# The expert layer of 128 of the 512 tokens by gathered expert rows, the dense expert passes on the other 384

## What is computed

```
q = (xt @ w_query).reshape(T, PEER_HEADS, 2, PEER_HALF)
s = einsum('thpd,pkd->thpk', q, sub_keys)             # scores of 2 x 128 keys
s_top, i_top = lax.top_k(s, K)                        # K = 16
cand = s_top[..., 0, :, None] + s_top[..., 1, None, :]
best, pos = lax.top_k(cand, K)                        # 16 experts of each head
eidx = index of the chosen pair (first key * 128 + second key)
g = softmax(best)
u = expert_u[eidx]                                    # rows, [T, heads, K, 1024]
a = gelu(einsum('thkd,td->thk', u, xb))
w = g * a
out = einsum('thk,thkd->td', w, expert_v[eidx])
```

## Time and profile before

| | us |
|---|---|
| median of three runs | 3341.32 |
| the profiled execution | 3339.1 |
| its span, first to last instruction | 3337.3 |
| stage A, from the trace | about 219 |
| stage W | about 465 |
| stage C | about 131 |
| between the passes | about 11 |
| stage V | about 705 |

### The profile page before, as it was taken

One profiled execution on the slowest core, in us unless ns is written; L12 is line 12 of the kernel. 1 busy time (PEld: TensorE's weight loads), 2 busy tenths in 40 slices (PEclk: granted clock), 3 DMA queues, 4 the chain that ended last, 5 costly groups with the idle time before them and its releaser, 6 DMA issues.

```text
span 3337.3 us, 38272 instructions
## 1 busy us (share of the span) xinstructions
PE 3069.8 (92%) x13740; PEld 2417.3 (72%) x13740; DVE 2045.0 (61%) x3267; ACT 1018.7 (31%) x1298; POOL 20.1 (1%) x19
## 2 busy tenths in 40 slices
PE   3966889999999999989999999769999998899997
PEld 2653458888888888878888888548887783478885
DVE  5456748975666663244444444487777647468886
ACT  3211434333333333232222222222222326322222
POOL 0001000000000000000000000000000000100000
...
GB/s 193 82 110 145 29 52 64 133 145 141 169 176 189 180 184 176 176 189 183 195 184 192 201 183 188 94 26 94 94 94 89 88 89 1 32 70 95 99 96 51
DMA packets 130786, 414.75 MB, mean 124 GB/s; under 512 B 7696, under 2 KB 73616, under 8 KB 98448
## 3 DMA queue, kind: packets, MB, share of 16 engines
...
## 4 chain that ended last, share of the span: by engine, by line
PE 87%; DVE 8%; ACT 2%; DMA 1%; issue 1%; POOL 0%; SPq 0%; ACTq 0%; DVEq 0%
PE ps L332 26%; PE ps L336 25%; PE ps L335 25%; PE ps L1793 3%; PE ps L1552 2%; PE ps L1970 1%; DVE sb_stats L1484 1%; DMA sb_stage<-w_ada_l 1%; DVE sb_ada_sum L1039 1%; PE ps L1735 1%; PE ps L1569 1%; DMA sb_xT<-x_l 1%; PE ps L1769 0%; PE ps L1997 0%; PE ps L1861 0%
## 5 line engine op out<-in xcount | busy, mean ns | idle before, releaser
L302 DVE TENSOR_TENSOR sb_wL<-sb_stage,sb_wH 128x2048 fp32r<-128x2048 f32 (+2 forms) x257 | 539.4, 2100 | 750.7 <-ACT sb_wH L297 750.2
L332 PE MATMUL ps<-sb_hL,sb_wH 128*128 128x512 f32 x2256 | 903.6, 401 | 73.9 <-DVE sb_hL L1338 32.6
L336 PE MATMUL ps<-sb_hH,sb_wH 128*128 128x512 f32 x2256 | 883.4, 392 | 0.0
L335 PE MATMUL ps<-sb_hH,sb_wL 128*128 128x512 f32 x2256 | 882.4, 391 | 0.0
L297 ACT ACTIVATE sb_wH<-sb_stage 128x2048 fp32r<-128x2048 f32 (+2 forms) x257 | 447.1, 1757 | 400.7 <-PE ps L332 350.0
L332 PEld LDWEIGHTS ps<-sb_hL,sb_wH 128*128 128x128 f32 x2256 | 426.1, 189 | 173.9 <-issue 70.3
L335 PEld LDWEIGHTS ps<-sb_hH,sb_wL 128*128 128x128 f32 x2256 | 426.6, 189 | 91.9 <-issue 5.8
L336 PEld LDWEIGHTS ps<-sb_hH,sb_wH 128*128 128x128 f32 x2256 | 425.7, 189 | 92.3
L332 PE MATMUL ps<-sb_waL,sb_wH 128*128 128x512 f32 x1024 | 404.3, 395 | 11.4 <-issue 11.4
L336 PE MATMUL ps<-sb_waH,sb_wH 128*128 128x512 f32 x1024 | 401.9, 392 | 0.0
L335 PE MATMUL ps<-sb_waH,sb_wL 128*128 128x512 f32 x1024 | 397.9, 389 | 0.0
...
## 6 DMA issues: line engine op xcount, KB each, us to landing
sb_stage<-u_l SPq DMA_DIRECT2D x64, 1024.0 KB, 4.9
sb_stage<-v_l SPq DMA_DIRECT2D x64, 1024.0 KB, 6.6
sb_stage<-up_l SPq DMA_DIRECT2D x44, 1024.0 KB, 4.8
g_scratch<-sb_ga ACTq DMA_DIRECT2D x64, 512.0 KB, 2.7
...
sb_wg<-w_scratch SPq DMA_DIRECT2D x32, 1024.0 KB, 7.2
sb_scr<-g_scratch SPq DMA_DIRECT2D x64, 512.0 KB, 3.4
sb_stage<-down_l SPq DMA_DIRECT2D x44, 512.0 KB, 3.5
```

What stands on the lines that cost most here:

```text
L302: dve.tensor_tensor(wL[k % SLOTS][:, 0:n], stage[k % STAGES][:, 0:n], wH[k % SLOTS][:, 0:n], ALU.subtract).then_inc(w_split, 1)
L332: m = pe.matmul(dst, lh, rl, start=first, stop=False)
L335: pe.matmul(dst, ll, rh, start=False, stop=False)
L336: return pe.matmul(dst, lh, rh, start=False, stop=last)
```

## The change

Of the 512 tokens the first 128 (`SP`) leave the dense passes, which go on with the other 384 (`TD`). Every matmul of the two passes has 384 columns in place of 512; `ga`, `g_scratch`, `waH`, `waL` and `wg` are a quarter smaller; the table of gates has 96 groups of 4 tokens in place of 128, so stage W has 24 steps in place of 32 and stage C 20 in place of 12.

For the 128 tokens each lies on a partition of its own. PE transposes their activations (16 full-precision matmuls with the identity), ACT copies them to `tok` (128x1024). DVE writes the 128 expert numbers of every token to `row_at`. Then come 128 rounds for `expert_u` and 128 for `expert_v`: in a round POOL issues an indirect DMA that gathers one row of 4 KB for each of the 128 partitions (512 KB) into one of two buffers `rows`. For `expert_u` DVE multiplies the rows with `tok` and sums along the row in one instruction (`row_dot`, with `accum_out`); for `expert_v` it adds the rows, times the gate, to `tok` (`row_sum`). Both are a SCALAR_TENSOR_TENSOR of 128x1024. The gather of round r waits until DVE has used round r-2. These DVE instructions stand in the order at fixed places: 10 behind the third and 10 behind the fourth block of stage A, 2 a step in stage W, 3 a step in stage C; in stage V 4 in each of the first two steps and then 2 a step up to step 61. At the end PE transposes `tok` back into the PSUM banks with 8 matmuls, and the final addition goes on as before.

Some semaphores are merged (`s_turn`, `s_wo`), without a change of order.

```
+SP = 128
+TD = T - SP
+SLOT_GROUPS = P // SP
+ROUNDS = PEER_H * TOPK // SLOT_GROUPS
-W_END = W_FIRST + T // 16
+W_END = W_FIRST + TD // 16
+ROUNDS_A, ROUNDS_W, ROUNDS_C, ROUNDS_V = 20, 8, 12, ROUNDS // 16
...
+            def row_dot(r, i=0, per=0):
+                dve.wait_ge(s_g[f"ld{r % 2}"], 16 * (r // 2 + 1) + 8 * per * i)
+                dve.scalar_tensor_tensor(rows[r % 2][:, :], rows[r % 2][:, :], 1.0, tok[:, :], ALU.mult, ALU.mult,
+                                         accum_out=column(row_act, r, i, per)).then_inc(s_g["used"], 1)
+            def row_sum(r, i=0, per=0):
+                dve.wait_ge(s_g[f"ld{r % 2}"], 16 * ((ROUNDS + r) // 2 + 1) + 8 * per * i)
+                dve.wait_ge(s_g["used"], ROUNDS + r + per * i)
+                dve.scalar_tensor_tensor(tok[:, :], rows[r % 2][:, :], column(row_act, r, i, per), tok[:, :],
+                                         ALU.mult, ALU.add).then_inc(s_g["used"], 1)
...
+                if tt == 1:
+                    row_places()
...
+                if tt >= 2:
+                    for r in range((tt - 2) * ROUNDS_A // 2, (tt - 1) * ROUNDS_A // 2):
+                        row_dot(r)
...
             with dve.Fori(0, (PEER_STEPS - W_END) // 4) as i:
                 for q in range(4):
                     split_lo(dve, C_PEER + W_END + 2 + q, CHUNK, i, 4)
+                    for r in range(ROUNDS_C * q // 4, ROUNDS_C * (q + 1) // 4):
+                        row_dot(ROUNDS_A + ROUNDS_W * (W_END - W_FIRST) // 4 + r, i, ROUNDS_C)
...
+            dve.wait_ge(s_g["gelu"], 1)
+            chain(dve.tensor_tensor(row_act[:, :], row_act[:, :], row_gate[:, :], ALU.mult))
+            chain(dve.memset(tok[:, :], 0.0))
...
                 for q in range(4):
                     peer_dve(2 + q, i)
+                    for r in range(ROUNDS_V // 4):
+                        row_sum(ROUNDS_V + ROUNDS_V // 4 * q + r, i, ROUNDS_V)
...
+            pool.wait_ge(s_g["at"], 1)
+            for r in range(2 * ROUNDS):
+                if r >= 2:
+                    pool.wait_ge(s_g["used"], r - 1)
+                pool.indirect_dma_start(rows[r % 2][:, :], None, A["u_rows" if r < ROUNDS else "v_rows"],
+                                        bass.IndirectOffsetOnAxis(ap=row_at[:, r % ROUNDS:r % ROUNDS + 1], axis=0)
+                                        ).then_inc(s_g[f"ld{r % 2}"], 16)
...
-                tile(C_PEER + s0, m, ps[:, 2 * (s0 % 2) + m, :], s_u["a"])
+                product(pe, C_PEER + s0, ps[:, 2 * (s0 % 2) + m, 0:TD], slice(m * P, (m + 1) * P), KT, 256,
+                        hH[:, :, SP:T], hL[:, :, SP:T], s_u["a"], m == 0)
...
-                        ins = three(pe, ps[:, d, :], wh[:, m, d * P:(d + 1) * P], wl[:, m, d * P:(d + 1) * P],
+                        ins = three(pe, ps[:, d, SP:T], wh[:, m, d * P:(d + 1) * P], wl[:, m, d * P:(d + 1) * P],
...
+            pe.wait_ge(s_g["used"], 2 * ROUNDS)
+            for d in range(KT):
+                pe.matmul(ps[:, d, 0:SP], tok[:, d * P:(d + 1) * P], both, start=True, stop=True
+                          ).then_inc(s_g["out"], 1)
```

More of the change, by code:

```diff
@@ L157, in build @@
             fromsel = sb("fromsel", [P, 3, T], scope=s4)
-            ga = [sb(f"ga{i}", [P, 2, T], scope=s4) for i in range(2)]
+            ga = [sb(f"ga{i}", [P, 2, TD], scope=s4) for i in range(2)]
+            rows = [sb(f"rows{i}", [P, D], scope=s4) for i in range(2)]
+            tok = sb("tok", [P, D], scope=s4)
+            row_at = sb("row_at", [P, ROUNDS], U32, scope=s4)
+            row_gate = sb("row_gate", [P, ROUNDS], scope=s4)
+            row_act = sb("row_act", [P, ROUNDS], scope=s4)
             with ExitStack() as s5:
@@ L195, in build @@
             dv = sb("dv", [P, TT, D], scope=s9)
+            sb("above", [P, D + D], scope=s9)
             rope_d = sb("rope_d", [P, 2, T], scope=s9)
@@ L669, in _ @@
                  dstH=hH, dstL=hL,
-                 ready=(s_wo1["added"], 0), mod_at=4)
+                 ready=(s_wo["added"], 0), mod_at=4)
             def keys_copy(t):
@@ L688, in _ @@
             keys_copy(15)
+            act.wait_ge(s_g["tok"], 1)
+            act.activation(tok[:, :], ps[:, 6:8, :].rearrange("p b n -> p (b n)"), ACT.Copy).then_inc(s_g["copied"], 1)
             def gate_exp(tt):
@@ L876, in _ @@
             norm("ffn1", lambda k: xT[:, k, :], KT, dstH=hH, dstL=hL,
-                 ready=(s_wo2["added"], 0), late=(s_wo2["added"], KT))
+                 ready=(s_wo["added"], KT), late=(s_wo["added"], 2 * KT))
             ffn_scalar(1, C_FFN2)
@@ L1167, in _, with column, row_places @@
             picks = pick_buffers()
+            def column(t, r, i, per):
+                return t[:, r:r + 1] if isinstance(i, int) else t[:, bass.ds(r + per * i, 1)]
+            def row_dot(r, i=0, per=0):
[7 more added lines that the diff above has]
+                                         ALU.mult, ALU.add).then_inc(s_g["used"], 1)
+            def row_places():
+                for g in range(SLOT_GROUPS):
+                    at, own = slice(g * SP, (g + 1) * SP), slice(g * ROUNDS, (g + 1) * ROUNDS)
+                    chain(dve.tensor_copy(row_gate[at, :], chosen[0:SP, 2, own]))
+                    op = dve.scalar_tensor_tensor(row_at[at, :], chosen[0:SP, 0, own], float(PEER_KEYS),
+                                                  chosen[0:SP, 1, own], ALU.mult, ALU.add)
+                    if g < SLOT_GROUPS - 1:
+                        chain(op)
+                op.then_inc(s_g["at"], 1)
+                dve.wait_ge(s_g["at"], 1)
             def key_indices(tt):
@@ L1255, in _ @@
                         split_lo(dve, C_PEER + W_FIRST + 2 + q)
+                for r in range(ROUNDS_W // 4):
+                    row_dot(ROUNDS_A + ROUNDS_W // 4 * q + r)
             n0 = chain.n
@@ L1263, in _ @@
                             split_lo(dve, C_PEER + W_FIRST + 2 + q, CHUNK, i, 4)
+                    for r in range(ROUNDS_W // 4):
+                        row_dot(ROUNDS_A + ROUNDS_W // 4 * q + r, i, ROUNDS_W)
             chain.n = n0 + 16 * ((W_END - W_FIRST) // 4 - 1)
@@ L1286, in _ @@
             dve.wait_ge(ld_const, 80)
-            dve.wait_ge(s_w["prod"], T // 4)
+            dve.wait_ge(s_w["prod"], TD // 4)
             rope_tables(2, lambda q: rope_d[:, q, :], posi[:, :], col("inv64"), col("sign64"), (7, 8))
-            peer_dve(0)
-            peer_dve(1)
+            dve.wait_ge(s_g["gelu"], 1)
+            chain(dve.tensor_tensor(row_act[:, :], row_act[:, :], row_gate[:, :], ALU.mult))
+            chain(dve.memset(tok[:, :], 0.0))
+            if SLOT_GROUPS == 2:
+                chain(dve.tensor_tensor(both, tab[:, IDENT, 0:SP], tab[:, IDENT, SP:P], ALU.add))
+            for s in range(2):
+                peer_dve(s)
+                for r in range(ROUNDS_V // 2):
+                    row_sum(ROUNDS_V // 2 * s + r)
             with dve.Fori(0, PEER_STEPS // 4 - 1) as i:
@@ L1781, in _ @@
             key_scores(15)
+            for k in range(KT):
+                for g in range(SLOT_GROUPS):
+                    dst = ps[g * SP:(g + 1) * SP, 6 + k // 4, k % 4 * P:(k % 4 + 1) * P]
+                    pe.matmul(dst, hH[:, k, 0:SP].bitcast(F32), tab[:, IDENT, :], start=True, stop=False)
+                    m = pe.matmul(dst, hL[:, k, 0:SP].bitcast(F32), tab[:, IDENT, :], start=False, stop=True)
+            m.then_inc(s_g["tok"], 1)
+            pe.wait_ge(s_g["copied"], 1)
             def selection(n, r):
```

127 lines of the change are left out of this document (66 added, 61 removed).

## The result

The changed kernel takes 3226.7 us (median of 4 runs, 3224.0 to 3229.8) against 3341.3 for the kernel before on the same chip: ratio 0.966, 95% interval 0.9648 to 0.9672. It is faster, by 115 us and not by the 183 forecast; the time lies inside the range. The profiled execution took 3225.9 us, 70 more than the sum that the prediction made for it.

What follows compares the result with a forecast made beforehand. The prediction took PE's matmuls to bound the kernel. Stage changes summed to 183 us less, so 3339.1 became 3156 in the profiled execution and 3158 us as median, with a range of 3070 to 3295.

Steps and rivals of the forecast that it cites:

- The weight loads, the rival with 0.02: All 384-column matmuls: they cost no less than a weight load, 0.19 us; V +30, total 3190 us; chance 0.02.
- signs of being wrong: W waiting for gathers, a product much over 1.4 us, V paced by gathers or late expert_v chunks, C at PE's pace.
- The bursts: Stage A, behind its third and fourth blocks: ten products each, two already landed, the others in two strands; 33.2 us.
- L: Every gather: time from a product's end over POOL's issue to the landing two rounds on; 6.2 us, bounds 3.4 and 9.5.
- The law around it: Stage C: three products a step on two buffers take 1.5 (L + 1.4) = 11.4 us a step.
- 1.5 us for all company: Part of L: 1.5 us added to each gather for the company of other transfers.
- POOL's preparation waits for the DVE instruction: Stage V: POOL waits for a running split of 2.29 us, so L = 8.5, about 3330 us; counted within chances 0.13 and 0.13.
- 30 us for each us of L: Stage C: each us by which L grows costs 30 us there.
- 557 + 12.6: Stage V: 8.7 us a step gives 557, plus 12.6 for the first two steps with four sums each; 570 us.
- L = 7.1: Stage V: from this L on, L + 1.33 passes PE's 8.4 us, and each further us costs 64 us more.
- Its own case: Whole kernel: L between 5 and 7.3 us, time 3105 to 3200 us; chance 0.5.
- the prediction's case between 7.3 and 8.5: Whole kernel: L between 7.3 and 8.5 us, time 3200 to 3340 us; chance 0.13.

Runs made afterwards that it cites:

- e1: The changed kernel without gathers, products and row sums, leaving only the dense passes on 384 columns; 2986.7 us.
- e8: The changed kernel, still on two buffers, with its expert_u rounds moved: none in stage A, 48 in W, 80 in C (four a step); 3257.2 us.
- e7: The changed kernel with DVE's split of a chunk cut into four instructions of 512 columns in stages C and V; 3204.8 us.
- e3: The changed kernel with four row buffers instead of two from round 68 on, same bytes and instructions; 3078.6 us.
- e2: The changed kernel without gathers; products and row sums run on buffers set to zero once; 3014.4 us.

## Why the prediction was right, and where it was short

*The matmuls.* Right: 0.174 us for 384 columns, steps of 8.3 to 8.4. The weight loads, the rival with 0.02, set nothing.

*Stage W.* Forecast 298, measured 295. PE's 11.9 is the floor (286 in e1); with full rows every other step takes some 12.9, and with quarter rows none does, so the 9 us above the floor are gathers, which the prediction had called hidden. DVE's waits for them in W (836 to 1131 us) are one of its own signs of being wrong:

```profile
DVE sb_rows L1192 <- DMA sb_rows<-u_rows,sb_row_at: 11.4, 13, 1.3
```

*The product.* Forecast 1.4 us, measured 1.15 from start to start. The sum's readout is there, and short (the changed kernel's first burst):

```profile
727.62 1.23 DVE L1192 SCALAR_TENSOR_TENSOR sb_rows<-sb_rows,sb_tok 128x1024 f32<-128x1024 f32 x1 [1.27 <-DMA sb_rows<-u_rows,sb_row_at]
728.77 0.08 DVE L1192 DVE_READ_ACCUMULATOR sb_rows<-sb_rows,sb_tok 128x1 f32 x1
```

*Stage A.* Step 20 begins at 836, forecast 844. The bursts lasted 28.8 and 29.1 us, forecast 33.2: in a quiet stage the loop was below the 6.2 taken.

*L, the term that failed.* The prediction put 6.2 us everywhere. The law around it was right (e8's plain step came within 3% of it); the size was not, and it is no one size. From the step of C, 13.0 / 1.5 less a product of 1.3, L is 7.4; from that of V, 9.4 less 1.3, it is 8.1; in the bursts it is about 5. Of the chain of waits of the changed kernel, first in stage A, then in C, then in V (start us, us):

```profile
729.13 4.65 DMA sb_rows<-u_rows,sb_row_at
```

```profile
1202.44 9.91 DMA sb_rows<-u_rows,sb_row_at
...
1213.98 5.67 DMA sb_rows<-u_rows,sb_row_at
...
1221.29 5.08 DMA sb_rows<-u_rows,sb_row_at
```

```profile
1505.66 6.23 DMA sb_rows<-v_rows,sb_row_at
...
1512.11 1.30 DVE sb_tok L1199
1513.41 0.26 issue
1513.67 8.62 DMA sb_rows<-v_rows,sb_row_at
```

(DMA here includes POOL's issue.) In C a gather that is issued beside a split, and with it the load of the next chunk, takes 8.2 us on average from its issue to its last packet, the others 5.3. In V the step decides more than the split. The issues of SP and of POOL around the two gathers above:

```profile
1499.00 0.39 SPq L297 DMA_DIRECT2D sb_stage<-v_l  x1
...
1509.45 0.45 SPq L467 DMA_DIRECT2D sb_wg<-w_scratch  x1
1510.15 1.42 SPq L297 DMA_DIRECT2D sb_stage<-v_l  x1
```

```profile
1505.66 2.74 POOL L1610 DMA_INDIRECT sb_rows<-v_rows,sb_row_at  x1 [0.74 <-DVE sb_tok L1199]
...
1513.67 2.75 POOL L1610 DMA_INDIRECT sb_rows<-v_rows,sb_row_at  x1 [1.51 <-DVE sb_tok L1199]
```

Both are issued beside a split, and one takes 6.23 us and the other 8.62. In every second step SP loads `w_scratch` just before the chunk, and the pair of gathers is issued 1 and 3 us behind the start of the chunk's load; in the other steps 5 and 7 us behind. In the first kind of step the first packet comes 3.0 and 2.6 us after the issue's end, in the second 0.7 (29 steps of each between 1450 and 2000 us, by the packet records; means). So a part of L in V comes with SP's loads, where the prediction had put 1.5 us for all company; no run takes them away by themselves, so that they are its cause is argued and not shown. Three things were missing in the 6.2, by the means of stage C and of V: 0.45 and 0.33 us of wake-up that had no term; an issue of 1.52 and 1.82 where 1.3 was taken; and 5.6 and 5.9 from the issue's end to the next use where 4.9 was taken. The prediction's mechanism "POOL's preparation waits for the DVE instruction" is real, and smaller than its 2.3 us a gather: in C it adds 0.7 and 1.0 us to two gathers of three (1.68 and 1.91 for 0.94), in V 1.8 us to one of two. The 22 us of e7 are what four pieces win back of it.

*What the size cost.* In C DVE needed 262 us and not 228: 34 us, and by the prediction's own price of 30 us for each us of L, 36 less 3 for the cheaper product. Its last product ended at 1394.6 and not at 1365. In V the first four steps were 5 us over the forecast and the others 39, 0.7 a step above the 8.7. (The prediction's 557 + 12.6 is 1 us too much, for the 12.6 counts from steps of 8.4.) The prediction had found the point from which V pays, L = 7.1, and with L = 6.2 put the DMA engines in its place; they were not what paced V, as e3 shows with 8.4 us a step at a share of 0.93, which is 7.8 us of the engines for the forecast's 8.25. Together: -8 in A, -3 in W, +35 in C, +4 in the gap, +44 in V, 72 us; the tail of the program took 2 less, which leaves the 70.

*What that makes of the forecast.* Its own case, L between 5 and 7.3 and a time of 3105 to 3200 us, did not come. L of 7.4 and 8.1 and a time of 3227 are the prediction's case between 7.3 and 8.5, which had a chance of 0.13, and V paced by gathers was one of its signs of being wrong. What was right is the way of the change, the terms beside L, and a range wide enough for the middle case.

*The gap.* Forecast 40, measured 44, for the reasons given: PE stands until the last product, the tables and the first split are through. e2, where the products end early, has 17.

The Trainium skill, "DMA: Bandwidth & Descriptors", section "Anatomy of one DMA — SWDGE (gpsimd) path", gives 2.0 us plus the bytes at 436 GB/s, 3.2 us here. The gathers that the bursts of stage A waited for took 4.2 to 5.7 us from the start of the issue to the product; for gathers of 128 rows the measurement decides.
